# Transposed x loaded in place, a smaller mask, the first lane chosen head by head, diagonals on ScalarE and the rotation summed by TensorE

## The reference, cut to what matters

```python
cq = apply_rope(cq.reshape(B, S, C_HEADS, 2, HEAD_DIM), cos, sin)      # concat[t1*c - t2*s, t2*c + t1*s]
# A: s = where(valid, q k^T * d**-0.5 + bias, -1e30); softmax; times v
# C: softmax(q1 k1^T) - lam * softmax(q2 k2^T), block-causal in chunks of 64, times v, rms norm
h = layer_norm(DEEPNORM_ALPHA * h + mix, ln1_g[l], ln1_b[l])
# PEER, per block of 128 tokens
q = (xb @ w_q).reshape(PEER_BLOCK, PEER_HEADS, 2, PEER_HALF)
s = jnp.einsum('thpd,hpnd->thpn', q, sub_keys)
sv, si = lax.top_k(s, 16)                       # two lists per head
cand = sv[:, :, 0, :, None] + sv[:, :, 1, None, :]
fs, fi = lax.top_k(cand, 16)                    # 16 experts of 16384
g = softmax(fs)
hid = gelu(einsum('td,thkd->thk', xb, u[experts]))
out = einsum('thk,thkd->td', g * hid, v[experts])
```

## Time and profile before

| | |
|---|---|
| median of three runs | 3905.95 us |
| the profiled execution's own time | 3898.55 us |
| its span, first to last instruction | 3896.7 us |
| PE (TensorE) busy | 2408.7 us (62%) |
| DVE (VectorE) busy | 2923.2 us (75%) |
| ACT (ScalarE) busy | 531.2 us (14%) |
| POOL (GpSimd) busy | 2397.6 us (62%) |
| moved by DMA | 1295.78 MB, 333 GB/s on the mean |

### The profile page before, as it was taken

How to read it: one execution, slowest core, us unless ns; L and a number is a source line. 1 busy time by engine, 2 the same in 40 slices (tenths; PEclk the granted TensorE clock), 3 DMA queues, 4 the chain that set the end, 5 groups by cost and what they waited for, 6 DMA issues and landing times. The chain is left out here.

```text
span 3896.7 us, 29311 instructions
## 1 busy us (share of the span) xinstructions
PE 2408.7 (62%) x8928; PEld 1667.8 (43%) x8928; DVE 2923.2 (75%) x5647; ACT 531.2 (14%) x1237; POOL 2397.6 (62%) x2052
## 2 busy tenths in 40 slices
PE   8899527786798617767598717687788815600000
PEld 6676412464585313345486413355576513200000
DVE  2311786788877896778888797788777797798889
ACT  2310001122211101112110101122210101100000
POOL 0000377776675677766676577776566577777775
PEclk9989769997798859888698958998799968955555
DMA  4234699999899889999899989999799988999998
GB/s 176 96 107 140 213 324 361 369 392 348 294 408 409 339 316 347 368 384 392 325 389 409 352 321 347 361 390 391 291 365 409 370 323 308 355 350 367 368 387 339
DMA packets 359900, 1295.78 MB, mean 333 GB/s; under 512 B 40512, under 2 KB 40768, under 8 KB 359744
## 3 DMA queue, kind: packets, MB, share of 16 engines
q0 software_dynamic: 294912, 1073.87, 72.9%
q1 hardware_dynamic: 64256, 217.94, 14.8%
q10 hardware_dynamic: 576, 2.10, 0.1%
HBM read 1291.65 MB, written 2.10 MB: 332 GB/s over the span
## 5 line engine op out<-in xcount | busy, mean ns | idle before, releaser
L1057 POOL DMA_INDIRECT ring<-in_peer_u,eidx x1024 | 1222.6, 1194 | 960.1 <-DVE eidx L1181 475.1
L1057 POOL DMA_INDIRECT ring<-in_peer_v,eidx x1024 | 1174.8, 1147 | 516.8 <-issue 288.1
L1094 DVE CUSTOM_DVE_ANT_0 ring<-ring,hp 128x1024 f32<-128x1024 f32 x1024 | 1236.4, 1224 | 266.0 <-DMA ring<-in_peer_u,eidx 254.1
L1099 DVE SCALAR_TENSOR_TENSOR acc<-ring,wgt,acc 128x1024 f32<-128x1024 f32 x744 | 949.2, 1290 | 123.4 <-DMA ring<-in_peer_v,eidx 101.2
L519 PE MATMUL bank<-xt,panel 128*128 128x256 f32 x4096 | 952.8, 392 | 33.7 <-ACT raw L854 8.5
L519 PEld LDWEIGHTS bank<-xt,panel 128*128 128x128 f32 x4096 | 804.1, 198 | 164.0 <-issue 27.0
L752 PE MATMUL bank<-ring,dg 128*128 128x512 f32 x1120 | 549.6, 632 | 497.2 <-ACT dg L826 363.7
L752 PEld LDWEIGHTS bank<-ring,dg 128*128 128x128 f32 x1120 | 208.9, 198 | 825.4 <-issue 578.6
L594 PE MATMUL bank<-dg,ex 128*128 128x128 f32 x640 | 112.8, 349 | 149.2 <-DVE dg L1341 84.5
L594 PEld LDWEIGHTS bank<-dg,ex 128*128 128x128 f32 x640 | 105.4, 257 | 161.3 <-issue 145.7
L715 PE MATMUL bank<-yt,panel 128*128 128x256 f32 x768 | 173.6, 379 | 0.0
(11 more groups left out here) (164 smaller groups left out, 1884.0 us busy)
## 6 DMA issues: line engine op xcount, KB each, us to landing
panel<-in_panels SPq DMA_DIRECT2D x368, 512.0 KB
ring<-in_peer_u,eidx POOLq DMA_INDIRECT x1024
ring<-in_peer_v,eidx POOLq DMA_INDIRECT x1024
work<-in_rel_bias SPq DMA_DIRECT2D x16, 512.0 KB
gb<-in_ln_g SPq DMA_DIRECT2D x8, 512.0 KB
gb<-in_ln_b SPq DMA_DIRECT2D x8, 512.0 KB
panel<-in_keys SPq DMA_DIRECT2D x16, 256.0 KB
work<-in_x SPq DMA_DIRECT2D x4, 512.0 KB, 5.2
```

Source lines behind the costliest of these rows:

```text
L1057: pool.indirect_dma_start(ring[:, n % RING, :], None, t_in["peer_u" if kind == "U" else "peer_v"], bass.IndirectOffsetOnAxis(ap=eidx[:, t, ...
L1094: v.tensor_tensor_reduce(row, row, hp[:, t, :], 1.0, 0.0, ALU.mult, ALU.add, hid[:, t, c:c + 1]).then_inc(used, 1)
L1099: stt(out=acc[:, t, :], in0=row, scalar=wgt[:, t, c:c + 1], in1=acc[:, t, :], op0=ALU.mult, op1=ALU.add).then_inc(used, 1)
```

## The change

x is laid out transposed on the host and loaded straight into `xt` with one DMA a half; in phases 0 and 1 nothing is turned. The load for phase 1 moves from the middle of phase 0's stage A to the end of phase 0's loads, behind a wait for the last query projection. In stage A the mask is a 64x64 block, placed before q times k. The diagonals of A and C are made by ScalarE; VectorE makes the inverses only, for the second map of C multiplied by the lambda. For the rotation VectorE makes both products, the sines with the opposite sign, and TensorE adds identity times the first and swap times the second into one bank, from which ScalarE copies q and k; the matmuls of unit 0 move from stage B to the start of stage C. In phase 0 the first lane is chosen for head 0 alone, then for head 1; the first gather waits for head 0's indices. The counts of the turning semaphores change accordingly.

```diff
             def load_x(s):
-                for t in range(TILES):
-                    first = (s * TILES + t) * P
-                    sp.dma_start(xn[:, t, :], t_in["x"][first:first + P, :]).then_inc(x_in[t], 16)
+                sp.dma_start(xt[:].rearrange("p c t -> p (c t)"), t_in["x"][s]).then_inc(x_in, 16)
...
-                if s == 0:
-                    sp.wait_ge(x_turned, 4)
-                    load_x(1)
                 for i in range(STAGE_PANELS["B"]):
...
+                if s == 0:
+                    sp.wait_ge(tq_ev, 16)
+                    load_x(1)
...
                     if kind == "A":
                         mm(sc[i][:, 0:k], ident, strip[:, u % 2, m, STRIP - k:STRIP], start=True, stop=False)
+                        mm(sc[i][0:CHUNK, k - CHUNK:k], ident[0:CHUNK, 0:CHUNK], maskblk[0:CHUNK, CHUNK:P],
+                           start=False, stop=False)
...
-                    mm(sc[i][:, k - P:k], ident, maskblk, start=False, stop=True).then_inc(s_done[kind], 1)
+                    if kind == "C":
+                        ins = mm(sc[i][:, k - P:k], ident, maskblk, start=False, stop=True)
+                    ins.then_inc(s_done[kind], 1)
...
-            def swap_qk(s, u):
+            def turn_qk(s, u):
                 n = s * UNITS + u
-                pe.wait_ge(qk_ev["C"], n + 1)
+                pe.wait_ge(rot_done, n + 1)
                 if u >= 2:
                     pe.wait_ge(o_ev["C"], n - 1)
-                mm(bank[1][:, :], swap, raw[:, u % 2].rearrange("p a t -> p (a t)"), start=True, stop=True
-                   ).then_inc(swapped, 1)
+                mm(bank[1][:, :], ident, rot[:, 0].rearrange("p a t -> p (a t)"), start=True, stop=False)
+                mm(bank[1][:, :], swap, rot[:, 1].rearrange("p a t -> p (a t)"), start=False, stop=True
+                   ).then_inc(turned, 1)
...
                 project_qk("C", s, 1)
-                swap_qk(s, 0)
                 inputs_b(s, 1)
...
+                turn_qk(s, 0)
                 scores("C", s, 0)
                 for u in range(UNITS):
                     weigh("C", s, u)
                     if u + 1 < UNITS:
-                        swap_qk(s, u + 1)
+                        turn_qk(s, u + 1)
                         scores("C", s, u + 1)
...
+            def take_rope(s, u):
+                n = s * UNITS + u
+                act.wait_ge(turned, n + 1)
+                copy(qt[:, u % 2, :], bank[1][:, 0:HALF])
+                copy(kt(s % 2, "C", u), bank[1][:, HALF:2 * HALF]).then_inc(rope_done, 1)
...
+            def diagonals(kind, s, u):
+                n = s * UNITS + u
+                for i in range(4):
+                    if i % 2 == 0:
+                        act.wait_ge(rinv_done[kind], n * 2 + i // 2 + 1)
+                    fn(dg[:, u % 2 * 4 + i, :], ident, ACT.Copy, scale=rinv[:, u % 2, i:i + 1]).then_inc(dg_done[kind], 1)
...
                 take_v("C", s)
+                take_rope(s, 0)
                 exps("C", s, 0)
                 for u in range(UNITS):
+                    diagonals("C", s, u)
                     take_weighed("C", s, u)
+                    if u + 1 < UNITS:
+                        take_rope(s, u + 1)
                     gelus((s, "C", u, 4))
...
-                if kind == "U" and k == 0 and t == 0:
+                if n == 0:
+                    pool.wait_ge(first_idx, 1)
+                elif kind == "U" and k == 0 and t == 0:
                     pool.wait_ge(peer_idx, s * LANES + head // 2 + 1)
...
+            def choose_first():
+
+                dve.wait_ge(scored, 2)
+                pick(0, 0, 0, 1, first_idx)
+                dve.wait_ge(panel_done, PANEL[(0, "K", 0)] + 1)
+                pick(0, 0, 1, 2, peer_idx)
...
-                tt(rot[:, 0], raw[:, u % 2], cs[:, 0, half].unsqueeze(1).broadcast_to(wide), ALU.mult).then_inc(*own.one())
-                dve.wait_ge(swapped, n + 1)
-                tt(rot[:, 1], bank[1][:].rearrange("p (a t) -> p a t", a=2),
-                   cs[:, 1, half].unsqueeze(1).broadcast_to(wide), ALU.mult).then_inc(*own.one())
-                step()
-                tt(qt[:, u % 2, :], rot[:, 0, 0, :], rot[:, 1, 0, :], ALU.add).then_inc(*own.one())
-                tt(kt(s % 2, "C", u), rot[:, 0, 1, :], rot[:, 1, 1, :], ALU.add).then_inc(rope_done, 1)
-                dve.wait_ge(rope_done, n + 1)
-                step()
+                if n:
+                    dve.wait_ge(turned, n)
+                for a in range(2):
+                    ins = tt(rot[:, a], raw[:, u % 2], cs[:, a, half].unsqueeze(1).broadcast_to(wide), ALU.mult)
+                ins.then_inc(rot_done, 1)
...
-            def diagonals(kind, s, u):
+            def inverses(kind, s, u):
                 n = s * UNITS + u
                 for m in range(2):
+                    cols = rinv[:, u % 2, 2 * m:2 * m + 2]
                     dve.wait_ge(e_done[kind], n * 4 + m * 2 + 2)
-                    v.reciprocal(rinv[:, u % 2, 2 * m:2 * m + 2], esum[:, u % 2, 2 * m:2 * m + 2]).then_inc(*own.one())
-                    step()
-                    for i in (2 * m, 2 * m + 1):
-                        if kind == "C" and m == 1:
-                            ts(dg[:, u % 2 * 4 + i, :], ident, rinv[:, u % 2, i:i + 1], small[:, 13:14],
-                               ALU.mult, ALU.mult).then_inc(dg_done[kind], 1)
-                        else:
-                            ts(dg[:, u % 2 * 4 + i, :], ident, rinv[:, u % 2, i:i + 1], None, ALU.mult
-                               ).then_inc(dg_done[kind], 1)
+                    if kind == "C" and m == 1:
+                        v.reciprocal(cols, esum[:, u % 2, 2 * m:2 * m + 2]).then_inc(*own.one())
+                        step()
+                        ts(cols, cols, small[:, 13:14], None, ALU.mult).then_inc(rinv_done[kind], 1)
+                    else:
+                        v.reciprocal(cols, esum[:, u % 2, 2 * m:2 * m + 2]).then_inc(rinv_done[kind], 1)
```

More of the change, by code:

```diff
@@ L311, in trunk @@
         pos_in = sem("pos_in")
-        x_in = [sem(f"x_in{t}") for t in range(TILES)]
+        x_in = sem("x_in")
         params_in = sem("params_in")
@@ L365, in trunk @@
         smax = {k: sem(f"smax_{k}") for k in "AC"}
+        rinv_done = {k: sem(f"rinv_done_{k}") for k in "AC"}
         dg_done = {k: sem(f"dg_done_{k}") for k in "AC"}
@@ L783, in _ @@
             for s in range(PHASES):
-                if s < 2:
-                    ready = [(x_in[t], 16 * (s + 1)) for t in range(TILES)]
-                else:
-                    ready = [(ln2_done, (s - 2) * TILES + t + 1) for t in range(TILES)]
                 if s:
@@ L790, in _ @@
                     pe.wait_ge(added, 2 * s - 1)
-                turn(xn, bank[0:2], ready, x_turned, x_taken, s * 4)
-                pe.wait_ge(x_taken, s * 4 + 4)
+                if s < 2:
+                    pe.wait_ge(x_in, 16 * (s + 1))
+                else:
+                    turn(xn, bank[0:2], [(ln2_done, (s - 2) * TILES + t + 1) for t in range(TILES)],
+                         x_turned, x_taken, (s - 2) * 4)
+                    pe.wait_ge(x_taken, (s - 1) * 4)
                 if s:
@@ L897, in stage_a @@
                 for u in range(UNITS):
+                    diagonals("A", s, u)
                     take_weighed("A", s, u)
@@ L1157, in choose @@
                 step()
-                top16([cand[:, a, :] for a in range(PAIRS)], left, fsh, fi, go, None)
-                ab4 = ab.rearrange("p (a c) b -> p a c b", c=2)
-                ts(ab4[:, :, 0, :], fi, 4, None, ALU.logical_shift_right).then_inc(*own.one())
-                ts(ab4[:, :, 1, :], fi, TOP - 1, None, ALU.bitwise_and).then_inc(*own.one())
+                top16([cand[:, a, :] for a in range(pa0, pb)], left[:, pa0:pb], fsh_, fi_, go, None)
+                ab4 = ab_.rearrange("p (a c) b -> p a c b", c=2)
@@ L1162, in choose @@
+                ts(ab4[:, :, 0, :], fi_, 4, None, ALU.logical_shift_right).then_inc(*own.one())
+                ts(ab4[:, :, 1, :], fi_, TOP - 1, None, ALU.bitwise_and).then_inc(*own.one())
                 step()
-                v.tensor_copy(abf, ab).then_inc(*own.one())
+                v.tensor_copy(abf_, ab_).then_inc(*own.one())
                 step()
-                flat = [P, LISTS * TOP, TOP]
-                tt(oh, abf.rearrange("p a b -> p (a b)").unsqueeze(2).broadcast_to(flat),
+                flat = [P, n_lists * TOP, TOP]
@@ L1171, in choose @@
                 step()
-                v.tensor_reduce(sel.rearrange("p a b -> p (a b)"), oh, X, ALU.add).then_inc(*own.one())
+                v.tensor_reduce(sel_.rearrange("p a b -> p (a b)"), oh_, X, ALU.add).then_inc(*own.one())
                 step()
-                sel4 = sel.rearrange("p (a c) b -> p a c b", c=2)
-                stt(out=ef, in0=sel4[:, :, 0, :], scalar=float(KEYS), in1=sel4[:, :, 1, :],
+                sel4 = sel_.rearrange("p (a c) b -> p a c b", c=2)
```

(7 more changed lines are left out.)

66 lines of the change are left out of this document (41 added, 25 removed).

## The result

The changed kernel took 3931.8 us (median of 7 runs, 3925.5 to 3939.8) and the kernel before, in as many runs, 3909.2: ratio 1.007, interval 1.0049 to 1.009. That is slower by 0.5% to 0.9%; I had forecast no change with 3906.5. The profiled execution took 3931.79 us; its span is 3930.0 us, 33.3 more than before.

A forecast was written before the change was run, and what follows sets the result against it. TensorE's chain was taken to bound phase 0 up to 441.4 us, streaming expert rows the rest. The terms summed to +0.5 us: 3899 profiled, 3906.5 as a median; likeliest range 3888 to 3925, wider 3872 to 3934.

The forecast's parts named there:

- x in phase 0: Start of phase 0: without the 16 transposes and 4 copies the first projection starts earlier, -4.5 us.
- The diagonals' delay: Stage A: ScalarE's diagonals queue behind copies of q and k; +1.55 us for phase 0 units 1 and 2, +5.2 in sum.
- Phase 0 up to the norm: Phase 0 before the choosing of experts: the terms for x, diagonals, mask and rotation together, about +6 us.
- The rotation in phase 1: Stage C of phase 1: 11.7 us from inversion to maximum against 13.3, -1.6 for three units; opening +3.5.
- The first gather: Sign to look for: the first expert row fetched near 424 plus about 6 us, 11 us earlier than 441.9.
- these end a whole lane ahead of stage A, so I cost this at nothing: Queue SP in phase 0's lanes: phase-1 panels held behind the last query projections, costed at nothing; uncovered 1.5 us.
- stages A of phases 1 to 3, +6.9: Diagonals there cost +0.7 us for three units and +0.6 for the first; with the mask +2.3 a phase, three times.
- With hops +2.4: Stage C of phase 0: two copies and four diagonals before weighing, +2.15, and +0.2; with hops +2.4 for two units.
- rival 2: TensorE's clock falls in some 28 pauses before weighing: 42 us slower, half of them 3927 us; chance 0.15.
- The mask, -2.7: Stage A of phase 0: the 64x64 block saves 0.17 us each for 16 on TensorE's chain, -2.7.
- The first lane, -11: Lane 1 of phase 0: choosing head by head gives indices 17 us earlier and gains 11 us, between 8 and 17.
- The rival of VectorE's time: After phase 0 VectorE's saved time counts one for one: 91 us at most, half 45, so 3850; chance 0.17.

The follow-up runs named there:

- base2: The kernel before, unchanged, profiled on the fourth chip, which has no late signals: ratio 1.001 (0.9985 to 1.0035).
- the first pair: The first measurement of the changed kernel (3931.8 us) and the kernel before (3909.2 us), chip not known: ratio 1.007.
- again: The changed kernel with no edit, run again on the second chip: 3852.3 us, ratio 1.000 to the kernel before.
- x_later4: The changed kernel with the load of x for phase 1 behind the first eight panels, fifth chip, with late signals: ratio 1.0029 to the kernel before.
- both2: The changed kernel with diagonals back on VectorE and x loaded behind the first eight panels, fifth chip: faster than the kernel before by 0.4% to 0.9%.
- no_diag: The changed kernel with the diagonals made by VectorE as before, second chip: ratio 0.9965 (0.9938 to 0.9991) to the kernel before.
- only_diag: The kernel before with only the diagonals moved to ScalarE, in stages A and C: ratio 1.0055 (1.003 to 1.0081).

## Why the prediction was wrong

**What held.** For x in phase 0 I had -4.5 us; it was -4.7 and -3.6. The diagonals' delay was put at +1.55 a unit: the units of stage A of phase 0 last 16.28 us with the diagonals alone and 14.63 before, +1.65. In phase 1 on a chip without late signals a unit takes 23.49 us against 22.69, +0.8 for the +0.7 forecast. Phase 0 up to the norm, forecast +6.0, grew by 6.2 in both columns of the table. The rotation in phase 1 was to take 11.7 us from inversion to maximum; it took 11.3, against 13.3 before:

```profile
990.30 0.15 DVE L1387 RECIPROCAL rinv<-esum 128x2 f32<-128x2 f32 x1
990.48 1.28 ACT L887 ACTIVATE dg<-cst,rinv 128x128 f32<-128x128 f32 x4 [2.86 <-DVE rinv L1387]
...
1000.25 0.92 PE L573 MATMUL bank<-work,qt 64*128 64x256 f32 x4 [0.74 <-ACT work L866]
1001.62 0.56 DVE L1373 TENSOR_REDUCE nmax<-bank 128x1 f32<-128x384 f32 x1 [6.17 <-PE bank L577]
```

The wait has moved from the swap to the maximum (6.17), as put. The first gather came 10.4 us earlier, forecast 11. The price of a diagonal is near that of the earlier trace rows: four in 1.28 us.

**The step that failed first: "these end a whole lane ahead of stage A, so I cost this at nothing".** The panels were indeed there in time for stage A. But the prefetch had a second consumer of its quiet time: the expert rows. Held back, 6 MB came in one burst in lane 2, where VectorE waits for rows anyway, and lanes 2 and 3, put at no change, grew by 10.1 us. I had asked whether the panels come too late, not what they push aside when they come. With the load of x behind them, three runs on chips without late signals give back 6.7 to 9.3 of the 10.1 us that lane 2 is longer there than in base2 (108.5, 106.3 and 105.9 for 115.2, with 105.1 in base2).

**The term that was mis-sized: stages A of phases 1 to 3, +6.9.** Between the second and fourth chip they measured -1.3, in the first pair +28.3, and the trace that I had was of the first pair. A unit of phase 1 grew by 4.9 to 6.3 us there, not by 0.7. The step that failed is that the sum gives every exchange between TensorE and ScalarE no more than its copies and a hop ("0.85 with the hop", "With hops +2.4"), and here single exchanges took up to 10.5 us. The kernel before had 56 late signals in that trace too, and I took none of them for what they are. Three were in plain sight: in phase 2 ScalarE takes over the projection of v 7.0 us after its last matmul (in the changed kernel 10.5; in `again`, on the second chip, 0.04). A path with one more exchange between TensorE and ScalarE, on which the unit's end hangs, would have more to lose. After the pauses TensorE ran at 1.2 GHz for 20 us of stage A of phase 1 (785.6 to 806.0 us, granted clock 0.50). In the whole stage TensorE is busy 91.6 us, against 79.5 before for nearly the same matmuls (352 and 348), and VectorE waits 16 us more for scores. That the diagonals are the part that matters most is shown (x_later4 against both2, 38 us). That it works through the added exchange and the clock is what the rows of phase 1 suggest; it was not tried apart, and the share of the clock differs from trace to trace. My rival 2, the clock, had this price, 21 to 42 us, with chance 0.15. But it took the pauses for the diagonals' own, in every unit from phase 0 on, and its sign, a granted clock in stage C well under 0.75, did not come (0.78). Its counterargument, that the stages A are dense, is what failed.

**The mask, -2.7.** It is no gain: a unit of phase 0 takes 14.75 us with it and 14.63 without (no_diag and base2), and 16.41 and 16.28 with the diagonals (again and only_diag). The 64x64 block moves TensorE on by less:

```profile
64.55 0.33 PE L569 MATMUL bank<-cst 64*64 64x64 f32 x2
64.81 0.49 PE L573 MATMUL bank<-work,qt 64*128 64x128 f32 x2
65.22 0.70 PE L568 MATMUL bank<-work,cst 128*128 128x256 f32 x2
```

0.26 us to the next matmul, for 0.32; the first maximum after weighing is 0.16 us earlier. But the four maxima of a unit spread over 4.11 us for 4.02, and the projection after them starts later. Why four blocks take longer together stays open; there was no run of the mask alone. With the term at +0.5 the sum would be 3 us higher.

**The first lane, -11.** This is near in size on a chip without late signals: 8.8 us are gained in lane 1 and 8.5 are left at the start of phase 1. On those with late signals lane 1 gains 1 to 2, since the wait for the gates takes the place of the one for rows.

So the forecast of no change is what the second chip showed (1.000), but partly by luck, as errors cancel: the burst there is made good by the stages A, B and C. In the first pair, the last index is 35.5 us later and I had +0.5. Three rows of the table make up that difference: 10.1 are the burst in lanes 2 and 3, which every chip has, 21.4 the stages A beyond the +6.9, and 4.4 the missing gain of lane 1. The last two were seen only on chips with late signals. The rival of VectorE's time falls: VectorE's saved products bring nothing (only_diag), and its saved waits for the swap come back as waits for scores.

## What to carry to other kernels

When a transfer is moved in a queue, sum up what the queue holds back behind it and where that burst will land; "it arrives in time" is only half of the question. Moving work from an engine that waits to one that stands in the chain costs even where the work is hardly slower, and it adds an exchange that can be late. Take the profile of both kernels on more than one chip before you explain a difference under 1%, and look in the trace for idle time that has no releaser.

## What was not expected of the hardware

In three of six sets of runs semaphores that TensorE raises are recorded up to 12.0 us late, 50 to 97 of some 870 recorded ones in an execution; in the other three, on two chips, none is. Several often arrive together: in the kernel before, three raisings of the projection of v, whose matmuls end 3.4 us apart, are recorded at 1674.48, 1674.58 and 1674.67. None is late or missing before the first gather of expert rows, though a sixth of TensorE's signals lie there; the first late one comes over 11 us after it. It happens while the DMA engines are busy all the time (DMA share 1.03 in the rows above), but they are as busy on the chips without it. VectorE has some too (13 to 58, up to 8 us, on the same chips), ScalarE none. The Trainium skill, page "Perfetto Trace Analysis", section "Summary: the profiler window per engine type", says that for TensorE both the actual end and the passing on of the semaphore are hidden from the window that the profiler reports. The trace agrees on the end: the matmul's window closes at 842.01, and nothing in it tells of the 3.2 us that follow. But the raising is recorded apart from it, at 845.20, just before ScalarE's copy at 845.22. So the time is lost before the recorded raising. Whether the matmuls or their signals are late can't be told, nor why, nor whether it happens where nothing is profiled.

The chips with late signals are also the slower ones for the kernel before, 3903 to 3929 us against 3859 to 3861. Single executions of one version on one chip spread by up to 55 us. In the profiled ones the last stretch of rows, from the last index to the end, takes 462 to 501 us, whatever the version. The stage times before it mostly repeat within a few us and are what the tables rest on.
